# Sums of squares and their spreads on TensorE in a two-layer decoder step: the squares as weights against the squares as the streamed side

## What is computed

```python
def rms_norm(x, g):
    xf = x.astype(jnp.float32)
    y = xf * lax.rsqrt(jnp.mean(xf * xf, axis=-1, keepdims=True) + NORM_EPS)
    return (y * g.astype(jnp.float32)).astype(x.dtype)

def l2_normalize(x):
    xf = x.astype(jnp.float32)
    return xf * lax.rsqrt(jnp.sum(xf * xf, axis=-1, keepdims=True) + L2_EPS)

def decoder_layer(x, l, prm, past, pos0, blocked):
    x = x + 0.5 * swiglu(rms_norm(x, prm['ffn1_norm'][l]), prm['ffn1_w_gu'][l], prm['ffn1_w_down'][l])
    h = rms_norm(x, prm['mix_norm'][l])
    ...
    q = rms_norm(a_q.reshape(B, T, NSA_HEADS, HEAD_DIM), prm['nsa_q_norm'][l]) * (HEAD_DIM ** -0.5)
    slc_new = jnp.stack([rms_norm(kv[:, :, 1, 0], kg[1]), kv[:, :, 1, 1]], axis=2)
    win_new = jnp.stack([rms_norm(kv[:, :, 2, 0], kg[2]), kv[:, :, 2, 1]], axis=2)
    ...
    dq = l2_normalize(dq.reshape(B, T, DN_HEADS, DN_DK)) * (DN_DK ** -0.5)
    dk = l2_normalize(dk.reshape(B, T, DN_HEADS, DN_DK))
    ...
    o_d = rms_norm(o_d.astype(x.dtype), prm['dn_out_norm'][l]) * jax.nn.silu(d_z.reshape(B, T, DN_HEADS, DN_DV))
    ...
    o_h = rms_norm(o_h.astype(x.dtype), prm['hg_out_norm'][l]) * jax.nn.sigmoid(r_og.reshape(B, T, HG_HEADS, HG_DV))
    ...
    x = x + merged @ prm['w_out'][l]
    x = x + 0.5 * swiglu(rms_norm(x, prm['ffn2_norm'][l]), prm['ffn2_w_gu'][l], prm['ffn2_w_down'][l])
```

## Time and profile before

| what | us |
|---|---|
| three runs, median | 3649.24 |
| three runs, least and most | 3645.81, 3649.37 |
| the profiled execution, its own time | 3651.84 |
| its span in the trace | 3650.0 |
| PE busy | 3337.8 (91%) |
| PEld busy | 2922.2 (80%) |
| POOL busy | 1285.5 (35%) |
| DVE busy | 1224.5 (34%) |
| ACT busy | 1090.5 (30%) |

### The profile page before, as it was taken

One profiled execution on the slowest core, in us unless ns is written; L12 is line 12 of the kernel. 1 busy time (PEld: TensorE's weight loads), 2 busy tenths in 40 slices (PEclk: granted clock), 3 DMA queues, 4 the chain that ended last, 5 costly groups with the idle time before them and its releaser, 6 DMA issues.

```text
span 3650.0 us, 70201 instructions
## 1 busy us (share of the span) xinstructions
PE 3337.8 (91%) x27660; PEld 2922.2 (80%) x27660; DVE 1224.5 (34%) x1939; ACT 1090.5 (30%) x1940; POOL 1285.5 (35%) x736
## 2 busy tenths in 40 slices
PE   7999899999778789999989998999997796889999
PEld 6888788768778677888878887887787785878887
DVE  3221201565333645321132211016633346452212
ACT  4332312342112223333233323214421122233322
POOL 3443323424221604334434343233342225133344
PEclk9999998998987979999999999989988778799999
DMA  3343322223002223233324333222230031322233
GB/s 138 117 140 92 121 75 81 80 81 105 27 1 102 67 91 116 77 101 91 102 86 149 102 96 125 73 86 75 86 103 12 7 112 67 110 86 89 95 95 114
DMA packets 109794, 326.05 MB, mean 89 GB/s; under 512 B 14866, under 2 KB 28178, under 8 KB 107026
## 3 DMA queue, kind: packets, MB, share of 16 engines
q1 hardware_dynamic: 109442, 321.29, 27.2%
q10 hardware_dynamic: 144, 1.86, 0.1%
HBM read 286.72 MB, written 36.39 MB: 89 GB/s over the span
## 4 chain that ended last, share of the span: by engine, by line
issue 46%; PE 31%; POOL 19%; DVE 1%; POOLq 1%; DMA 1%; ACT 1%; DVEq 1%; ACTq 0%; SPq 0%
PE pair L1629 16%; POOL w_lo L1603 15%; PE pair L728 2%; PE pair L261 2%; PE pair L119 1%; PE pair L380 1%; POOL arena L890 1%; PE pair L409 1%; PE pair L400 1%; POOL mixed L1265 1%; POOL mixed L1264 1%; PE pair L689 1%; PE pair L355 1%; PE pair L1005 1%; POOL arena L1264 1%
## 5 line engine op out<-in xcount | busy, mean ns | idle before, releaser
L1603 POOL TENSOR_TENSOR w_lo<-raw,w_hi 128x1024 f16<-128x1024 f32 x340 | 743.4, 2198 | 1339.6 <-ACT w_hi L1599 1339.6
L1689 PE MATMUL pair<-arena,w_hi 128*128 128x260 f16 x4096 | 699.5, 278 | 35.3 <-DVE arena L2089 16.8
L1689 PE MATMUL pair<-arena,w_lo 128*128 128x260 f16 x2048 | 569.5, 278 | 0.0
L1629 PE MATMUL pair<-h_hi,w_hi 128*128 128x260 f16 x1792 | 503.3, 281 | 7.8 <-ACT z_out L1653 7.8
L1599 ACT ACTIVATE w_hi<-raw 128x1024 f16<-128x1024 f32 x340 | 348.7, 1051 | 536.4 <-PE pair L1689 417.7
L1629 PE MATMUL pair<-h_lo,w_hi 128*128 128x260 f16 x1792 | 502.3, 280 | 0.0
L1629 PE MATMUL pair<-h_hi,w_lo 128*128 128x260 f16 x1792 | 501.9, 280 | 0.0
L1680 PE MATMUL pair<-h_hi,w_hi 128*128 128x260 f16 x1728 | 479.5, 278 | 16.9 <-DVE h_lo L2079 16.9
L1689 PEld LDWEIGHTS pair<-arena,w_hi 128*128 128x128 f16 x4096 | 405.3, 99 | 97.0 <-POOL w_lo L1603 17.9
L1680 PE MATMUL pair<-h_lo,w_hi 128*128 128x260 f16 x1728 | 477.9, 277 | 0.0
L1680 PE MATMUL pair<-h_hi,w_lo 128*128 128x260 f16 x1728 | 477.9, 277 | 0.0
(11 more groups left out here) (333 smaller groups left out, 5123.6 us busy)
## 6 DMA issues: line engine op xcount, KB each, us to landing
raw<-in_w_up SPq DMA_DIRECT2D x180, 512.0 KB, 3.2
raw<-in_w_z SPq DMA_DIRECT2D x84, 512.0 KB, 3.4
raw<-in_w_dn SPq DMA_DIRECT2D x64, 512.0 KB, 3.5
raw<-in_w_mg SPq DMA_DIRECT2D x48, 512.0 KB, 3.8
parked_z<-z_out SPq DMA_DIRECT2D x80, 260.0 KB, 4.0
arena<-parked_z SPq DMA_DIRECT2D x6, 2080.0 KB, 7.9
raw<-in_w_dn SPq DMA_DIRECT2D x32, 384.0 KB, 3.1
raw<-in_w_wb SPq DMA_DIRECT2D x24, 512.0 KB, 3.8
```

The costliest lines, as they stand in the source:

```text
L1603: e.tensor_tensor(w_lo[s % 4], raw[s % 2], w_hi[s % 4], ALU.subtract).then_inc(w_split, 1)
L1629: mm = pe.matmul(bank(a)[:, 0:HALF], w[f % 4][:, k, :], xx[:, k, a * HALF:(a + 1) * HALF], start=(k == 0 and p == 0), stop=(k == KD - 1 an ...
L1689: mm = pe.matmul(out, w[s % 4][:, kw, :], xx(kx), start=(first and i == 0 and p == 0), stop=(last and i == len(ks) - 1 and p == 2))
```

## The change

`SUMS`, `PIECES` and `spread` go. `row_sums` makes four matmuls per block: the weights are a 128x32 selector from a new tile `picks`, of zeros with one column of ones (for "n" two columns, each with ones on half the partitions), and 130 columns of squares are streamed. Piece q goes to partitions 32q to 32q+31 of bank 7, and all blocks of a norm accumulate there, block i on row 32q+i. Root and reciprocal are then taken once per norm on 128x130, and a drain stands behind the reciprocal. `spread_rows` makes four matmuls per block (eight for "n"): the weights are one identity column, broadcast, over 64 partitions, and the 130 columns of reciprocals are streamed; the order is q = 0, 2, 1, 3.

In a big norm DVE adds seven squares and not eight. PE sums `sq_sum` first and adds the eighth square to it from its own buffer. A one-element root (`junk`) is put ahead of each small norm's first square, and ahead of the seventh block of the projection in front of a big norm. In "o" the product with gain and gate now stands ahead of the reciprocal; behind the spread DVE has one multiply. The selectors are set once at the program's start.

```diff
+def row_sums(pe, out, pick, src, first, last):
+    for q in range(4):
+        mm = pe.matmul(out[32 * q:32 * q + 32, 0:QN], pick, src[:, QN * q:QN * q + QN], start=first, stop=last,
+                       skip_group_check=True)
+    return mm
+
+def spread_rows(pe, pair, rows, ident, i, groups=1):
     w = P // groups
-    for j, c0, c1 in PIECES:
-        a = c0 // HALF
+    for q in (0, 2, 1, 3):
+        o = slice(64 * (q // 2), 64 * (q // 2) + 64)
         for g in range(groups):
-            f = factors[:, groups * j + g:groups * j + g + 1].to_broadcast([P, w])
-            mm = pe.matmul(pair[w * g:w * g + w, a, c0 - a * HALF:c1 - a * HALF], f,
-                           ident[:, c0 - SUMS[j]:c1 - SUMS[j]], start=True, stop=True)
+            at = 32 * q + groups * i + g
+            mm = pe.matmul(pair[w * g:w * g + w, q // 2, QN * (q % 2):QN * (q % 2) + QN],
+                           ident[o, at:at + 1].to_broadcast([64, w]), rows[o, 0:QN], start=True, stop=True)
     return mm
...
     for i in range(n):
         pe.wait_ge(S_.sem, S_.at(f"{name}q{i}", l))
-        for j, c in enumerate(SUMS):
-            mm = pe.matmul(m["bank"](7)[:, at(i, j):at(i, j) + groups], sqr[:, i % 2, c:c + P], src, start=True, stop=True)
-        mm.then_inc(*T_.step(f"{name}s{i}"))
+        pick = m["pick1"][:, 31 - i:63 - i] if groups == 1 else m["pick2"][:, 30 - 2 * i:62 - 2 * i]
+        row_sums(pe, m["bank"](7), pick, sqr[:, i % 2, :], i == 0, i == n - 1).then_inc(*T_.step(f"{name}s{i}"))
...
+    if not first:
+        e.activation(m["junk"], m["eps"][:, :], ACT.Sqrt)
     for i in range(first, len(bufs)):
...
+    for i, b in enumerate(bufs):
+        if after(i) is not None:
+            e.wait_ge(S_.sem, S_.at(f"{name}q{i}", l))
+            e.scalar_tensor_tensor(b, b, gain(i), after(i), ALU.mult, ALU.mult)
     e.wait_ge(S_.sem, S_.at(f"{name}d", l))
-    e.reciprocal(m["rstd"][:, 0:w], m["rstd"][:, 0:w]).then_inc(*V_.step(f"{name}r"))
+    e.reciprocal(m["rstd"][:, 0:QN], m["rstd"][:, 0:QN])
+    e.drain().then_inc(*V_.step(f"{name}r"))
     for i, b in enumerate(bufs):
         e.wait_ge(T_.sem, T_.at(f"{name}b{i}", l))
         h = m["halves"](b)
-        e.scalar_tensor_tensor(h, h, gain(i), m["both"](2 + i % 2), ALU.mult, ALU.mult)
         if after(i) is None:
-            e.drain().then_inc(*V_.step(f"{name}n{i}"))
+            e.scalar_tensor_tensor(h, h, gain(i), m["both"](2 + i % 2), ALU.mult, ALU.mult)
         else:
-            e.drain()
-            e.tensor_tensor(b, b, after(i), ALU.mult).then_inc(*V_.step(f"{name}n{i}"))
+            e.tensor_tensor(h, h, m["both"](2 + i % 2), ALU.mult)
+        e.drain().then_inc(*V_.step(f"{name}n{i}"))
...
-                pe.wait_ge(sum_done, 8 * (3 * l + s) + KD)
-                for j, c in enumerate(SUMS):
-                    mm = pe.matmul(bank(7)[:, j:j + 1], sq_sum[:, c:c + P], ones[:, 0:1], start=True, stop=True)
-                mm.then_inc(ss_done, 1)
+                pe.wait_ge(sum_done, 7 * (3 * l + s + 1))
+                row_sums(pe, bank(7), pick1[:, 31:63], sq_sum, True, False)
+                pe.wait_ge(sq_done, 8 * (3 * l + s + 1))
+                row_sums(pe, bank(7), pick1[:, 31:63], sq[:, 1, :], False, True).then_inc(ss_done, 1)
                 pe.wait_ge(inv_done, 3 * l + s + 1)
-                spread(pe, pair[3], ident, rstd[:, 0:5]).then_inc(inv_spread, 1)
+                spread_rows(pe, pair[3], rstd, ident, 0).then_inc(inv_spread, 1)
...
                 for b in range(KD):
+                    if b == 6:
+                        act_e.activation(junk, eps[:, :], ACT.Sqrt)
                     act_e.wait_ge(proj_ready, 8 * (3 * l + 1) + b + 1)
                     split_hi(act_e, l, AT_OUT + b, b)
                     square(l, 1, b, b % 2)
```

More of the change, by code:

```diff
@@ L720, in norm_sums @@
 def norm_sums(pe, l, m, T_, S_, name, n, sqr, groups=1):
-    at = lambda i, j: groups * (len(SUMS) * i + j)
-    src = m["ones"][:, 0:1] if groups == 1 else m["bones"][:, 0:P:P // groups]
     for i in range(n):
         pe.wait_ge(S_.sem, S_.at(f"{name}q{i}", l))
-        for j, c in enumerate(SUMS):
-            mm = pe.matmul(m["bank"](7)[:, at(i, j):at(i, j) + groups], sqr[:, i % 2, c:c + P], src, start=True, stop=True)
-        mm.then_inc(*T_.step(f"{name}s{i}"))
+        pick = m["pick1"][:, 31 - i:63 - i] if groups == 1 else m["pick2"][:, 30 - 2 * i:62 - 2 * i]
+        row_sums(pe, m["bank"](7), pick, sqr[:, i % 2, :], i == 0, i == n - 1).then_inc(*T_.step(f"{name}s{i}"))
 def norm_spreads(pe, l, m, T_, V_, name, n, groups=1, fill=None):
-    w = groups * len(SUMS)
     for i in range(n):
         pe.wait_ge(V_.sem, V_.at(f"{name}r" if i < 2 else f"{name}n{i - 2}", l))
-        spread(pe, m["pair"][2 + i % 2], m["ident"], m["rstd"][:, w * i:w * i + w],
-               groups).then_inc(*T_.step(f"{name}b{i}"))
+        if groups > 1:
+            pe.sem_inc(m["turns"], 1)
+        spread_rows(pe, m["pair"][2 + i % 2], m["rstd"], m["ident"], i, groups).then_inc(*T_.step(f"{name}b{i}"))
         if fill:
@@ L747, in norm_tensor, with norm_squares @@
     norm_spreads(pe, l, m, T_, V_, name, n, groups)
-def norm_squares(e, l, T_, S_, name, bufs, sqr, first=0):
+def norm_squares(e, l, m, T_, S_, name, bufs, sqr, first=0):
+    if not first:
+        e.activation(m["junk"], m["eps"][:, :], ACT.Sqrt)
     for i in range(first, len(bufs)):
@@ L1479, in hybrid_step_kernel @@
         rstd = sb("rstd", NBLK)
+        picks = sb("picks", 63 + 62 + 1)
+        pick1, pick2, junk = picks[:, 0:63], picks[:, 63:125], picks[:, 125:126]
         mixed = sb("mixed", 12 * N)
@@ L1983, in ffn @@
                                          sg[:, q:q + 1, :], ACT.Copy).then_inc(act_hi_done, 1)
-                with act_e.Fori(0, 2) as r:
+                for r in range(2):
                     for b in range(4):
+                        if 4 * r + b == 6:
+                            act_e.activation(junk, eps[:, :], ACT.Sqrt)
                         for j in range(2):
@@ L2027, in _ @@
             dve.memset(eps[:, :], EPS)
-            dve.memset(small[:, :], 0.0).then_inc(setup, 1)
+            dve.memset(small[:, :], 0.0)
+            dve.memset(picks[:, :], 0.0)
+            dve.drain().then_inc(setup, 1)
+            dve.memset(pick1[:, 31:32], 1.0)
+            dve.memset(pick2[0:HD, 30:31], 1.0)
+            dve.memset(pick2[HD:P, 31:32], 1.0)
             dve.sem_inc(gu_free, 4)
@@ L2063, in _ @@
             dve.drain()
-            for k in range(KD):
+            for k in range(KD - 1):
                 add_square(k + 1, k % 2)
@@ L2068, in norm @@
                 dve.wait_ge(std_done, 3 * l + s + 1)
-                dve.reciprocal(rstd[:, 0:5], rstd[:, 0:5]).then_inc(inv_done, 1)
+                dve.reciprocal(rstd[:, 0:QN], rstd[:, 0:QN]).then_inc(inv_done, 1)
                 dve.wait_ge(inv_spread, 3 * l + s + 1)
@@ L2098, in residual @@
                 dve.drain()
-                with dve.Fori(0, KD // 2) as r:
-                    for j in range(2):
-                        dve.wait_ge(proj_ready, 8 * (3 * l + s) + 2 * r + j + 1)
-                        xk = x[:, bass.DynSlice(2 * r + j, 1), :].rearrange("p k (a n) -> p (k a) n", a=2)
-                        dve.scalar_tensor_tensor(xk, both(j), scale, xk, ALU.mult, ALU.add).then_inc(x_done, 1)
-                        add_square(8 * (3 * l + s + 1) + 2 * r + j + 1, j)
+                for k in range(KD):
+                    dve.wait_ge(proj_ready, 8 * (3 * l + s) + k + 1)
+                    xk = halves(x[:, k, :])
+                    dve.scalar_tensor_tensor(xk, both(k % 2), scale, xk, ALU.mult, ALU.add).then_inc(x_done, 1)
+                    if k < KD - 1:
+                        add_square(8 * (3 * l + s + 1) + k + 1, k % 2)
             def merge(l):
```

35 lines of the change are left out of this document (16 added, 19 removed).

## The result

The changed kernel takes 3538.34 us (median of 4 runs, 3537.37 to 3545.46) against 3647.95 for the kernel before on the same chip: a ratio of 0.9704, 95% interval 0.9692 to 0.9716. (They differ by 4.6 us more than the medians: the profiled execution of before, at 3651.84, was slower than its own median.)

What follows compares the result with a forecast made beforehand. PE was taken as the bound, with the norms on its path. Small norms 66 us and big norms 17.4 make 83.6, less about 2: 82 off 3651.84, and 2.6 for the profiled execution, gives 3567; range 3543 to 3610.

Steps and rivals of the forecast that it cites:

- That norms are on PE's path: Chain of waits: sums and spreads of the norms (2% and 1%) stand on the path with PE's fill, not beside it.
- Sums: Small norms' sums: ACT sets the pace, 0.71 us per block at half clock; n 6.3, l 10.0, o 4.4 us faster.
- G: Time of the new group of four sum matmuls on PE, estimated at 0.42 us at full and 0.70 at half clock.
- Spreads: Small norms' four 64-row matmuls: 2.0 us at half clock, 1.0 at full; n 1.4, l 1.9, o 2.4 us faster.
- rival 4: No overlap in a group of sums, 2.2 us each: 3638, slower than before from 2.44 on; chance 0.09.
- Big norms: Last square to first multiply takes 4.3 us, 3.65 less, in four norms 14.6; with the loop's head 17.4 in all.
- the layer loop's head: Big norm there keeps its table load, and DVE's way around the loop may end last: 2.8 us gained.
- rival 3: The clock stays at 2.4 GHz through the norms, as streaming 130 columns could hold it up: 3538; chance 0.08.
- changes of shape: PE's changes of tiling mode at the norms: 2 us counted in all; by the skill's drain rule 5 to 10 us.
- the last line of the table: Last multiply in "o", changes of shape and all else: 1.2 us of gain in the forecast.
- Rival 1: Only two of the four column groups overlap in the sums, 1.23 us per group at half clock: 3585; chance 0.17.
- Rival 2: Weights come late for the fill behind shorter n and l norms: 3583 if half the sums' gain goes, 3600 if all; chance 0.08.

## Why the prediction was right and where it failed

*That norms are on PE's path*: right. All that was taken from them came out of the span.

*Sums*: right, mechanism and size. G was 0.66 at half clock, 0.43 at full (0.70 and 0.42 were taken), a block's pitch 0.71 with ACT as the pace setter, and the loads ahead of the squares cost their 1.5 us; 50.2 us in both. That it agrees to the tenth is luck: the forecast doubled the first layer, but the second layer's "n" sums had taken 10.44 before and not 12.37, which lost 1.9 us, and small gains elsewhere made up for it.

*Spreads*: the step that failed. It read "two streams of 0.43 and four loads, 2.0 at half clock, 1.0 at full". Two things are wrong in it. The sum doesn't follow from its parts: 2.0 needs loads of 0.285 each, while rival 4 takes "about 0.1" for the same loads, and with that the sum would have been 1.26. And loads are not added to streams. At half clock the load of a whole matmul takes as long as its stream (two records of 0.215), but it lies beside it, and the loads of the two halves lie beside each other (16 of them in 1.82 us, the PEld row of "o" above). So 1.26 would have been near the mark by luck. Measured are 1.24 at half clock alone, 1.04 in a row of four, DVE's waits included, 0.87 from PE's own pace, and in "l" at full clock

```profile
867.54 0.72 PE L127 MATMUL pair<-rstd,const 64*128 64x130 f32 x8
```

0.72 busy, 0.5 less per spread than before instead of 0.24. That is 20.3 us in the small norms, some 5 of the 6.4 in the big ones (two of the five spreads there ran at full clock, 0.72), and so most of the difference of 33. The rows to see it were on the table: a record of the sums with one streamed column and the records of the spread, with 128 columns for the most part, took the same 0.21 us. Had loads and streams added up, the spread's records would have been longer by a stream. The same error stood in rival 4's 2.2 us for four sums in turn, where 1.73 was measured.

*Big norms*: the add, the group of sums, root and reciprocal as forecast; the spread as above. At the layer loop's head 4.6 us were gained, not 2.8: DVE's way around the loop, which ended last before, no longer has an add behind it.

*The rest*: the clock's part, which the forecast left to rival 3, is small. In the changed kernel the granted clock is 0.50 in the sums and in the spreads of "o", so that rival's condition was not met there, though its time was: that agreement is chance. The fill behind "n" got 2.3 us from a clock that came back sooner, and the two big norms' spreads at full clock about 1 us; but from the "l" sums to the first spread it is 23.3 and 23.2 us, where it was 22.4 and 22.9. No loss of 5 to 10 us for changes of shape shows either: the last line of the table came out above the forecast. 1.6 us of it were not traced further.

*Rival 1* is refuted: G is 0.66 at half clock, not 1.23; the four groups work at the same time. *Rival 2* shows only in a trace of it: the HGRN mixer's start waits for `parked_z` in the changed kernel's chain, and its stretch to the first sum grew by 2.3 us, 1.5 of it the load. What is left is less than what this stretch varies by between the kernels here, so its price is not shown.

*The range* was too narrow below, because the spread's lower bound (0.7) was used for full clock only, and the sum's band was drawn around the error.

## What to carry to other kernels

Before adding a weight load to a stream, look in the trace for two matmuls with equal weights and very different numbers of streamed columns: if their records take the same time, the load sets the price, and a stream that is no longer than the load is free. Stream the long operand and keep the weights narrow, so that idle row or column groups can be used: without the column groups the kernel was 28 us slower, without the row halves 16.5. The rest of the 110 us is not the streaming alone; the dropped add (16) and the moved multiply (11) are in it. When a stage becomes cheap, ask again who paces it: the multiply was worth 11 us, and not 3, only because PE no longer hid it. And a small instruction put ahead of a stage to load a table early costs its full time where the engine isn't idle: here 14 to 16 us over eight norms, of which the loads themselves make 12.

## What the runs showed of the hardware

- A float32 matmul leaves two records. At half clock each takes 0.21 us with 128 weight columns, whether 1, 65 or 128 columns are streamed, and 0.217 with 130; with 32 weight columns, half the streamed columns in twice the matmuls take the same time (2.61 in "o"). So the longer of load and stream counts, not their sum.
- Four matmuls on four 32-column groups take 0.66 us at half clock and 0.43 at full, start and end included, where the stream of one alone is 0.43 and 0.22; four in turn through the whole array take 1.73 at half clock. Two 64-row halves overlap in full, loads included, also when they don't alternate in the program.
- The granted clock was 0.60 to 0.84 in the "n", "l" and "o" sums through the whole array that were looked at, 0.50 in the narrow groups, with gaps in between, and 0.50 to 0.52 in the sums of the earlier trace rows, with PE busy all the time on one-column streams, but 0.64 in the second layer's "n" of that kernel. What raised it is not shown.
